# The second product of an MLP in seven half-width products instead of eight, with every low part on GpSimd

## The reference

```python
def squared_relu_mlp(h, w1, w2):
    return jnp.square(jax.nn.relu(h @ w1)) @ w2

def reference(x, ...):
    for i in range(DEPTH):
        ...
        x = x + y
        x = x + squared_relu_mlp(rms_norm(x, norm_mlp[i]), mlp_w1[i], mlp_w2[i])
    return x
```

## Time and profile before

| | |
|---|---|
| runs | 2807.37, 2807.53, 2809.55 us; median 2807.53 |
| span of the profiled execution | 2812.2 us, first to last instruction; no other time of that execution is shown |
| busy in it | PE 2726.8 (97%), PEld 2197.8, DVE 1037.2 (37%), ACT 1082.5 (38%), POOL 1387.4 (49%) |
| mean granted TensorE clock | 0.991 of 2.4 GHz |

### The profile page before, as it was taken

How to read it: one execution, slowest core, us unless ns; L and a number is a source line. 1 busy time by engine, 2 the same in 40 slices (tenths; PEclk the granted TensorE clock), 3 DMA queues, 4 the chain that set the end, 5 groups by cost and what they waited for, 6 DMA issues and landing times.

```text
span 2812.2 us, 37295 instructions
## 1 busy us (share of the span) xinstructions
PE 2726.8 (97%) x14594; PEld 2197.8 (78%) x14594; DVE 1037.2 (37%) x1936; ACT 1082.5 (38%) x1640; POOL 1387.4 (49%) x1074
## 2 busy tenths in 40 slices
PE   7999999999998999999899998999999999899999
PEld 5977678888765788888788887888888977688887
DVE  4035431113495522113777774311123044522112
ACT  4355442224346433224333444422234355533221
POOL 3566544454446354445535351544545576545443
PEclk9999999999999999999999999999999999999999
DMA  4331122323322123233311110223233322132232
GB/s 125 98 83 53 46 90 90 105 92 101 96 56 69 53 93 102 90 103 91 84 46 46 46 46 31 90 90 105 96 98 89 106 53 68 46 105 91 90 104 75
DMA packets 271884, 227.82 MB, mean 81 GB/s; under 512 B 29204, under 2 KB 259348, under 8 KB 271748
## 3 DMA queue, kind: packets, MB, share of 16 engines
q1 hardware_dynamic: 260880, 216.29, 25.4%
q10 hardware_dynamic: 10868, 9.66, 1.5%
HBM read 223.62 MB, written 2.30 MB: 80 GB/s over the span
## 4 chain that ended last, share of the span: by engine, by line
PE 91%; DVE 4%; ACT 2%; POOL 1%; issue 1%; DMA 0%; ACTq 0%; DVEq 0%; POOLq 0%
PE bank L1877 50%; PE bank L1786 20%; PE bank L1943 5%; PE bank L2170 2%; PE bank L2310 1%; PE bank L1918 1%; PE bank L1831 1%; PE bank L1996 1%; PE bank L2012 1%; POOL w_lo L578 1%; PE bank L1980 1%; PE bank L2097 1%; PE bank L2026 1%; PE bank L1973 1%; PE bank L2125 0%
## 5 line engine op out<-in xcount | busy, mean ns | idle before, releaser
L578 POOL TENSOR_TENSOR w_lo<-raw,w_hi 128x512 fp32r<-128x512 f32 x808 | 1080.9, 1367 | 1064.9 <-ACT w_hi L725 1064.9
L725 ACT ACTIVATE w_hi<-raw 128x2048 fp32r<-128x2048 f32 x202 | 385.5, 1908 | 456.9 <-PE bank L1877 423.3
L1877 PE MATMUL bank<-h_hi,w_hi 128*128 128x512 f32 x1024 | 400.8, 391 | 0.0
L1877 PE MATMUL bank<-h_hi,w_lo 128*128 128x512 f32 x1024 | 398.4, 389 | 0.0
L1877 PE MATMUL bank<-h_lo,w_hi 128*128 128x512 f32 x1024 | 398.4, 389 | 0.0
L1877 PE MATMUL bank<-g_hi,w_hi 128*128 128x512 f32 x1024 | 398.3, 389 | 0.0
L1877 PE MATMUL bank<-g_lo,w_hi 128*128 128x512 f32 x1024 | 398.3, 389 | 0.0
L1877 PE MATMUL bank<-g_hi,w_lo 128*128 128x512 f32 x1024 | 398.3, 389 | 0.0
L1786 PE MATMUL bank<-h_hi,w_hi 128*128 128x512 f32 x776 | 317.3, 409 | 10.1 <-POOL w_lo L578 7.2
L1786 PE MATMUL bank<-h_lo,w_hi 128*128 128x512 f32 x776 | 310.7, 400 | 0.0
L1786 PE MATMUL bank<-h_hi,w_lo 128*128 128x512 f32 x776 | 308.1, 397 | 0.0
(11 more groups left out here) (269 smaller groups left out, 3833.7 us busy)
## 6 DMA issues: line engine op xcount, KB each, us to landing
raw<-in_mlp_w SPq DMA_DIRECT2D x128, 1024.0 KB, 5.2
raw<-in_a_w_in SPq DMA_DIRECT2D x48, 512.0 KB, 5.1
raw<-in_c_w_in SPq DMA_DIRECT2D x32, 512.0 KB, 5.5
raw<-in_a_w_in SPq DMA_DIRECT2D x12, 1024.0 KB, 5.2
raw<-in_b_w_in SPq DMA_DIRECT2D x18, 256.0 KB, 4.4
raw<-in_a_w_out SPq DMA_DIRECT2D x4, 1024.0 KB, 4.8
raw<-in_b_w_in SPq DMA_DIRECT2D x4, 1024.0 KB, 5.4
arena<-bias_scratch ACTq DMA_DIRECT2D x16, 256.0 KB, 3.6
```

The lines of the kernel that those rows point to most:

```text
L578: ins = nc.gpsimd.tensor_tensor(w_lo[s][:, k, :], raw[s][:, k, :], w_hi[s][:, k, :].bitcast(F32), ALU.subtract)
L725: nc.scalar.activation(w_hi[s][:], raw[s][:], ACT.Copy).then_inc(w_hi_done, 1)
L1877: mm = nc.tensor.matmul(lin_bank[j][:], w[s][:, c, P * j:P * j + P], a[:, c, :], start=c + z == 0, stop=c == CT - 1 and z == 2)
```

## The change

Each down chunk, an output of 256 features by 512 tokens, is regrouped by a Strassen scheme of seven products: weights, hidden values and outputs are taken as 2 x 2 blocks (two halves of the features, two halves of the tokens, even and odd hidden tiles). Seven products of 12 matmuls with 256 columns (four pairs of hidden tiles times the three parts) stand in place of two tiles of 24 with 512. For that DVE makes sums of weights from `raw` (`summed_weights`: 1024, 512 and 512 columns, L1314 to L1319), ACT rounds these too (L784, 2048 columns), and POOL makes seven low parts of 512 columns per down chunk (three of weights, four of sums) in place of four. DVE also makes four sums of hidden values per pair of tiles (256 columns each), ACT rounds three of them in one instruction (768) and DVE makes their low parts (768). The results are added to `x` in eight additions of 256 columns (`add_part`) in place of two of 512, and two of PE's products wait until DVE has read what its bank held. ACT's rounding of the chunk ahead moves from behind both tiles of a pair to between them. All loops over the quarters are written out.

The pieces of the diff below are, in this order, POOL's split of a down chunk, ACT's rounding and its order in the up chunks, DVE's waits for weight sums, an odd tile and the order in both phases, and PE's product.

```diff
+            def split_halved(n):
...
+                pool.wait_ge(w_hi_done, v - 1)
+                of_weights(0).then_inc(w_lo_done, 1)
+                pool.wait_ge(w_hi_done, v)
+                of_sums(1).then_inc(w_lo_done, 1)
+                of_weights(2).then_inc(w_lo_done, 1)
+                of_sums(3).then_inc(w_lo_done, 1)
+                of_sums(2).then_inc(w_lo_done, 1)
+                of_weights(3).then_inc(w_lo_done, 1)
+                of_sums(0).then_inc(w_lo_done, 1)
...
+            def rounding(n):
...
                 nc.scalar.activation(w_hi[s][:], raw[s][:], ACT.Copy).then_inc(w_hi_done, 1)
+                if halved(n):
+                    act.wait_ge(ws_added, 3 * s_value[n])
+                    nc.scalar.activation(ws_hi[s][:], w_sum[s], ACT.Copy).then_inc(w_hi_done, 1)
...
+                    for p in range(4):
+                        squares(Q, p, 0)
+                        even_high(Q, p)
+                        if p < 3:
+                            round_ahead(n + p)
+                        squares(Q, p, 1)
+                        odd_high(Q, p)
+                    round_ahead(n + 3)
...
+            def summed_weights(n):
...
+                dve.wait_ge(raw_loaded[s], raw_value[n])
+                if n >= 2 and halved(n - 2):
+                    dve.wait_ge(w_lo_done, lo_value[n - 2])
...
+            def odd_tile(Q, T, p):
+
+                g, u = 8 * Q + 2 * p, 4 * Q + p
+                relu(Q, T, p, 1)
+                dve.wait_ge(gsq_done, g + 2)
+                nc.vector.tensor_tensor(pieces[:, 5, :], pieces[:, 4, :], pieces[:, 0, :], ALU.subtract).then_inc(gt_done, 1)
+                nc.vector.scalar_tensor_tensor(pieces[:, 6, :], pieces[:, 4, :], -1.0, pieces[:, 2, :], ALU.mult,
+                                               ALU.subtract).then_inc(gt_done, 1)
+                dve.wait_ge(gt_done, 4 * u + 3)
+                nc.vector.scalar_tensor_tensor(pieces[:, 7, :], pieces[:, 6, :], -1.0, pieces[:, 3, :], ALU.mult,
+                                               ALU.subtract).then_inc(gt_done, 1)
+                low(by_half(g_lo[:, 2 * p + 1, :]), pieces[:, 3:5, :], by_half(g_hi[:, 2 * p + 1, :]), 3 * u + 2)
...
+                    for p in range(4):
+                        even_tile(Q, T, p)
+                        odd_tile(Q, T, p)
+                        if p == 3:
+                            first_parts(Q, 0)
+                        odd_sums(Q, p)
+                        if p in (1, 2):
+                            summed_weights(n + p + 3)
...
+            def down(li, Q, n, X, d, m):
...
+                add_part(d, 2 * d + 1, 0, 3, ALU.subtract, part_added)
+                if m is not None:
+                    low_x(m, 2 * d)
+                    sum_square(m, 2 * d)
+                if d < 2:
+                    summed_weights(n + d + 2)
+                dve.wait_ge(lin_done, tile0[n + d] + 2)
...
+            def half_product(out, w, g, start, ready):
+
+                for p in range(4):
+                    if ready is not None:
+                        pe.wait_ge(gl_done, ready + 3 * p)
...
+                half_product(A, weight(0), hidden(0, 0), True, g[0]).then_inc(part_done, 1)
+                pe.wait_ge(w_lo_done, v + 2)
+                half_product(B, weight_sum(1), hidden(0, 1), True, None).then_inc(part_done, 1)
+                pe.wait_ge(w_lo_done, v + 3)
+                half_product(C, weight(2), hidden(1, 0), True, g[1]).then_inc(part_done, 1)
+                pe.wait_ge(w_lo_done, v + 4)
+                pe.wait_ge(part_added, 6 * u + 2)
+                half_product(B, weight_sum(3), hidden(1, 1), False, None).then_inc(part_done, 1)
...
```

More of the change, by code:

```diff
@@ L31 @@
 CW = 256
+HALF = TOK // 2
 EPS = 1e-6
@@ L112, in trunk, with halved @@
         raw_value.append(at[n % 2])
+    def halved(n):
+        return CHUNKS[n][0] == "mlp" and CHUNKS[n][2] % 8 >= 4
+    hi_value, lo_value, s_value = [], [], []
+    for n in range(N):
+        hi_value.append((hi_value[-1] if n else 0) + (2 if halved(n) else 1))
+        lo_value.append((lo_value[-1] if n else 0) + (7 if halved(n) else 1))
+        s_value.append((s_value[-1] if n else 0) + halved(n))
     def added(li, mlp):
@@ L536, in chunk, with mlp_chunk @@
                             load(n, r[:, :, c:c + HD], rows(b_w_in[0], (a + 4 * s) * HD, HD))
[L538 to L550, removed]
+            def mlp_chunk(n, i, q, k):
+                sp.wait_ge(w_lo_done, lo_value[n - 2])
+                if k < 4:
+                    load(n, raw[n % 2][:], rows(mlp_w1[i], q * DM + k * CW, CW))
+                else:
+                    load(n, raw[n % 2][:], rows(mlp_w2[i], (k - 4) * CW, CW, CT, q * DM))
             sp.dma_start(com[:], masks[0:COMMON_MASKS * P, :].rearrange("(k p) n -> p k n", p=P)).then_inc(const_loaded, 16)
@@ L559, in _ @@
                     chunk(k)
-                with sp.Fori(0, QUARTERS) as q:
-                    mlp_chunks(i, n_mlp, q)
+                for k in range(8 * QUARTERS):
+                    mlp_chunk(n_mlp + k, i, k // 8, k % 8)
             for b in range(NB):
@@ new lines, in mlp @@
+            def mlp(li, i, m):
+                for q in range(QUARTERS):
+                    n, _, Q, X = quarter(li, q)
+                    for p in range(4):
[6 more added lines that the diff above has]
+                    round_ahead(n + 3)
+                    if q < QUARTERS - 1:
+                        for k in range(4, 8):
+                            round_ahead(n + k)
+                    else:
+                        residual(n + 4, X, m)
@@ L1266, in mlp @@
[L1266 to L1269, removed]
+                for q in range(QUARTERS):
+                    n, T, Q, X = quarter(li, q)
+                    for p in range(4):
[6 more added lines that the diff above has]
+                            summed_weights(n + p + 3)
+                    last = q == QUARTERS - 1
+                    for d in range(4):
+                        down(li, Q, n + 4, X, d, m if last else None)
+                    if last and m is not None:
+                        dve.wait_ge(x_added, X + 8)
+                        low_x(m, CT - 1)
+                        sum_square(m, CT - 1)
```

258 lines of the change are left out of this document (163 added, 95 removed).

## The result

The changed kernel takes 3040.49 us (median; 3038.17 to 3044.34, 4 runs) against 2808.54 (2807.37 to 2810.43, 4 runs): 1.082 times as long, 95% interval 1.081 to 1.084. The prediction was 3040.

The account below looks back on a forecast made before the run. PE was taken as the bound in the MLP's sixteen quarters, half the span. Span 2812.2 plus 216 for quarters, 13 for layers' last and 4 for first quarters gives 3045; the median lies 4.7 below: 3040 us, range 2920 to 3110.

Parts of the forecast that it names:

- The cause: In the MLP, DVE instructions reading two SBUF inputs take turns with POOL's trains; 3040 us, chance 0.80.
- The walk: Step-by-step timing of one MLP quarter from PE's first up matmul, ending at 100.6 us against 87.04.
- Its prices: Under a POOL train, a 512-column DVE turn costs 1.7 us; POOL loses 0.2 at 256, 0.7 at 768 columns.
- the marks named: Expected trace signs: PE idle stretches, DVE's 256-column sums at 1 us or more, 512-column at 1.3, granted clock below 0.991.
- The stalls: PE's waits in a quarter, before up tile 6 and in the down chunks: 16.4 us in all.
- the clock: After each 8.7 us stall PE runs at 1.2 GHz, losing up to 3.0 us; costed at nothing, upper bound 48 us.
- tile 7's 0.4: In the first down chunk PE waits another 0.4 us for tile 7's low part, there at 59.0.
- the prediction's reason: DVE, its time set by POOL and ACT, holds D1 and D2, so D0's later end, up to 3.0 us, costs nothing.
- the next step of the walk: D3's `raw` loads once POOL is through with D1, 5.2 us; DVE's sums follow, PE stalls 3.1 in D2.
- PE's gain: Down chunks of 84 matmuls with 256 columns take 10.06 us against 10.88: 3.3 us a quarter, 52 in all.
- Rival B: In the MLP, DVE and POOL do not hold each other up: 13 us faster, 2795 us; chance 0.07.
- Rival D: Clock stays low in each down chunk and POOL's strided pieces are longer: 3150 us; chance 0.08.

Follow-up runs that it names:

- e1: Changed kernel with one operand of each of DVE's sums and low parts read from unused PSUM, values not computed rightly; 2810.37 us.
- e2: Kernel before the change, with each 512-column matmul of the down chunks issued as two of 256; 2850.23 us.
- e8: e5 with one operand of each of DVE's sums and low parts read from PSUM, multiplied by zero, values not computed rightly; 2799.44 us.
- e3: Changed kernel with ACT's rounding of the raw chunk ahead put back behind both tiles of a pair; 2969.18 us.
- e12: Changed kernel with weight sums' low parts on DVE, ACT's rounding behind both tiles, and weight sums spread singly between down-chunk additions; 2908.71 us.
- e5: Changed kernel with ACT's rounding behind both tiles of a pair and DVE's weight sums spread over the down chunks' additions; 2965.20 us.
- e10: Changed kernel without low parts of weight sums, ACT's rounding behind both tiles, weight sums spread chunk to chunk in one block; 2880.41 us.
- e6: Changed kernel with each of POOL's seven pieces of a down chunk made in two instructions of 256 columns; 3021.70 us.

## Why the prediction was right

**The cause.** That DVE's two-input SBUF instructions take turns with POOL's was read from two places in the trace of before. e1 removed only that and took the whole loss with it.

**The walk.** Times in the quarter, predicted and, less 560.08, measured:

| event | predicted | measured |
|---|---|---|
| tile 5's first sum over | 42.3 | 41.6 |
| relu of tile 6 starts, DVE's list over | 52.4 | 51.7 |
| low part of tile 6 there | 55.7 | 54.9 |
| additions that D1 waits for | 71.5 | 71.6 |
| additions that D2 waits for | 84.7 | 83.5 |
| quarter ends | 100.6 | 99.5 |

Its prices held, from one start to the next: 1.46 (of L1347 to L1350) and 1.40 for a turn at 256 columns (1.46 assumed), 1.71 at 512 (1.7), 1.96 at 768 (1.96), POOL's losses 0.18, 0.44 and 0.69 (0.2, 0.45, 0.7). The Trainium skill, SBUF — State Buffer, section Who interferes with whom, has the holder keep the port for its whole instruction, which would be a loss of 0.69 to an instruction of 512 columns. The trace does not agree: the loss is 0.44 there, and 0.69 only beside 768 columns. Of the marks named, two fell short. The sums of 256 columns were to have a mean of 1 us or more: in after those of an odd tile have 932, 1235 and 1155 ns, but the even tile's (L1338) 447. And the 512 weight sums' mean was too low, 1180 and 1144 ns by their groups where 1300 was the least expected: in this quarter half of them, those of D0 and D1, take 0.69 with POOL's train over, and half 1.67.

**The stalls** were 2.0, 6.4, 1.5 and 1.7, 11.6 in all, where the walk had 2.5, 8.7, 0.4 with 1.7, and 3.1, 16.4 in all. Most of the difference is the clock, which was costed at nothing. Behind the 2.0 us stall eight matmuls of tile 6 start 0.43 apart instead of 0.23, at a granted clock of 0.50, TensorE's lower level of 1.2 GHz; behind the 6.4 us one, 63 matmuls take 9.60 us instead of 7.5, at 0.78 on average. That is some 1.8 and 2.0 us more of PE's own time. The first comes out of D0's stall, which ends with DVE anyhow. The second makes D0 end later (tile 7's 0.4 is gone in it), and here the prediction's reason, that DVE's time is set by POOL and ACT, does not hold: the chain goes through these 63 matmuls to the addition at 624.62, for which DVE waited, and behind it stand the sums that D1's stall hangs on. What saves the forecast is the next step of the walk: D3's `raw`, asked for at 631.48 when POOL was through with D1, took 5.0 us, so it was there 0.2 us before its sums began at 636.65, and in every middle quarter 0.2 to 0.6. Without the low clock D2's additions could have come hardly earlier. So the clock did not move the quarter's end by much, as forecast; this is read from the traces, and no run took the low clock alone away. What it also had wrong is that only the long stalls would show the lower clock; the one of 2.0 did too, while those of 1.5 and 1.7 were followed by matmuls at full pace (36 in 4.50, 132 in 15.90).

**PE's gain**, 3.3 a quarter, is 3.0 to 3.4 by the paces of e1 (300 in 35.82), e2 and e8: right.

**The ends.** 16 quarters at 12.4 are 199 us where 216 were forecast. The rest of the 225 us in the MLPs, 26, falls to the layers' first and last quarters, for which the walk had 17. The loss between the MLPs had no term. It is 4 us in after and 2 in e3, but 16 to 18 in the six other kernels with POOL's seven pieces, and 10 in e12, which has only three. In the traces PE waits at the three MLP ends for the mixer's first pieces from POOL in after too, but 5.0 us in all against 10.6 in e1 and 12.1 in e5; what spares after and e3 was not tested. Rival B's 2795 was wrong by this term, although its sum inside the MLP (13) was near the 15.8 measured.

So that 3040 came within 0.5 us of 3040.49 is luck, for the terms are not that close: -17 in the steady quarters against +9 in the first and last, +4 between the MLPs, -2 ahead of the first, and a median that lies 1 above its span, where 5 below was assumed. Rival D, a clock that stays low and slow strided pieces, had no part: pieces of weights and of sums have the same mean of 1491 ns.

## What to carry to other kernels

A sum of busy times says nothing where two engines exclude each other. Before putting an elementwise step with two SBUF inputs on DVE beside a POOL train, price it by the turn that the trace shows (here 1.4 to 1.7 us for 0.4 to 0.7 us of work), and lay the list against the time until the next tile is due. Fewer columns on PE bought at most 48 us here, for seven low parts a chunk on POOL in place of four and all the sums on DVE: test such a change first with the conflicting operands taken from PSUM, as in e8; if even this gives 0.3%, the order is not worth tuning. And where an edit shortens one partner's waits, look first which of the two the chain passes through.

## What the runs showed of the hardware that I had not expected

- TensorE's clock fell behind a stall of only 2.0 us (eight matmuls of 512 columns 0.43 apart, granted clock 0.50), but not behind stalls of 1.5 and 1.67 us in the same quarter, nor behind one of 2.10 us in e10 (at 504.50, granted clock 1.00, 36 matmuls in 4.52). The stall's length alone does not tell it.
- Two POOL instructions of 256 columns take 1.40 us for one of 512 with 1.26 to 1.29: POOL's busy time rose by 102 us, from 1708.8 to 1811.1 in e6.
- Halving POOL's piece shortened the means of DVE's instructions by only 6 to 15% (1099 to 1030 ns, 1155 to 1016, 932 to 793), not by half a piece, about 0.6 us.
- DVE reading one operand from PSUM by a `scalar_tensor_tensor` keeps its full pace beside POOL's train (422 ns at 256 columns and 686 at 512 in e8).
